# Where RMSNorm's 1/rms is applied in a one-core hybrid layer: on x before its transposes, or on q, k, v and the LRU's tiles after the projection

## What is computed

```
h    = x * rsqrt(mean(x*x) + eps) * mix_norm_g          # RMSNorm per token
proj = h @ w_in                                         # 1024 -> 2560
xr, yg, q, k, v = split(proj)                           # 512 channels each
xr   = causal_conv4(xr) + b                             # per channel, along tokens
y_lru = rg_lru(xr) * gelu(yg)                           # gates, scan along tokens
q, k = rms_norm(q), rms_norm(k)                         # per head of 64
y_attn = attention(q, k, v)                             # 8 heads, ALiBi slopes
x = x + concat(rms_norm(y_lru), rms_norm(y_attn)) @ w_out
```

## Time and profile before

| what | value |
|---|---|
| median of three runs | 306.27 us |
| span of the profiled execution, first to last instruction | 304.5 us |
| what lies around the span, against the median of the runs | 1.8 us |
| PE busy | 298.2 us (98%) |
| DVE busy | 231.5 us (76%) |
| ACT busy | 175.8 us (58%) |
| transfers | 52.20 MB, mean 171 GB/s |

### The profile page before, as it was taken

How to read it: one execution, slowest core, us unless ns; L and a number is a source line. 1 busy time by engine, 2 the same in 40 slices (tenths; PEclk the granted TensorE clock), 3 DMA queues, 4 the chain that set the end, 5 groups by cost and what they waited for, 6 DMA issues and landing times.

```text
span 304.5 us, 5577 instructions
## 1 busy us (share of the span) xinstructions
PE 298.2 (98%) x2008; PEld 274.0 (90%) x2008; DVE 231.5 (76%) x410; ACT 175.8 (58%) x304; POOL 4.0 (1%) x21
## 2 busy tenths in 40 slices
PE   8899999999999999999999999999999999999995
PEld 8788998898988789999999999999999999999994
DVE  2998597798799767887787778777777778777765
ACT  6975598997756376854445545555444544555420
POOL 4000000000000000000000000000000000000000
PEclk9999999999999999999999999999999999999999
DMA  7999943033307701655365455355464554300003
GB/s 229 425 420 424 377 145 138 2 138 138 140 9 263 282 2 23 238 208 225 140 220 194 144 194 213 140 212 199 146 243 161 157 223 171 138 0 0 0 0 139
DMA packets 7981, 52.20 MB, mean 171 GB/s; under 512 B 896, under 2 KB 896, under 8 KB 2080
## 3 DMA queue, kind: packets, MB, share of 16 engines
q1 hardware_dynamic: 7776, 51.38, 45.4%
q0 software_dynamic: 192, 0.64, 0.5%
HBM read 50.98 MB, written 1.05 MB: 171 GB/s over the span
## 4 chain that ended last, share of the span: by engine, by line
PE 93%; DMA 2%; DVE 2%; ACT 1%; issue 0%; SPq 0%; ACTq 0%
PE bank L901 29%; PE bank L902 28%; PE bank L905 28%; DMA raw<-in_stream_dram 2%; PE bank L977 1%; DVE x_tok L893 1%; PE bank L990 1%; PE bank L1096 1%; PE bank L1095 1%; PE bank L966 1%; PE bank L1089 1%; PE bank L997 1%; PE bank L998 1%; PE bank L1115 0%; ACT p_T L498 0%
## 5 line engine op out<-in xcount | busy, mean ns | idle before, releaser
L901 PE MATMUL bank<-h_hi,w_hi 128*128 128x256 f32 x416 | 118.3, 284 | 0.3 <-DVE h_lo L823 0.3
L905 PE MATMUL bank<-h_hi,w_lo 128*128 128x256 f32 x416 | 117.7, 283 | 0.0
L902 PE MATMUL bank<-h_lo,w_hi 128*128 128x256 f32 x416 | 117.7, 283 | 0.0
L590 DVE TENSOR_TENSOR w_lo<-raw,w_hi 128x1024 fp32r<-128x1024 f32 x93 | 112.3, 1217 | 3.3 <-ACT w_hi L321 3.1
L321 ACT ACTIVATE w_hi<-raw 128x1024 fp32r<-128x1024 f32 x87 | 90.8, 1051 | 2.7 <-PE bank L905 1.8
L901 PEld LDWEIGHTS bank<-h_hi,w_hi 128*128 128x128 f32 x416 | 79.7, 192 | 3.0 <-issue 1.8
L902 PEld LDWEIGHTS bank<-h_lo,w_hi 128*128 128x128 f32 x416 | 79.7, 192 | 0.8
L905 PEld LDWEIGHTS bank<-h_hi,w_lo 128*128 128x128 f32 x416 | 79.7, 192 | 0.0
L543 ACT ACTIVATE xc<-bank,par 128x256 f32<-128x256 f32 x44 | 24.9, 566 | 87.7 <-PE bank L905 87.7
L849 DVE SCALAR_TENSOR_TENSOR xc<-bank,par,xc 128x255 f32<-128x255 f32 x44 | 21.2, 482 | 34.5 <-ACT xc L543 34.5
L901 PE MATMUL bank<-w_hi,act_hi 128*128 128x512 f32 x88 | 34.6, 393 | 0.0
(11 more groups left out here) (156 smaller groups left out, 302.6 us busy)
## 6 DMA issues: line engine op xcount, KB each, us to landing
raw<-in_stream_dram SPq DMA_DIRECT2D x46, 1024.0 KB, 4.8
x_tok<-in_x_dram SPq DMA_DIRECT2D x2, 512.0 KB, 3.8
raw<-in_stream_dram SPq DMA_DIRECT2D x2, 512.0 KB, 7.2
out_dram<-x_tok SPq DMA_DIRECT2D x4, 256.0 KB, 2.0
p_T<-in_gates_dram POOLq DMA_DIRECT2D x1, 512.0 KB, 9.3
par<-in_params_dram POOLq DMA_DIRECT2D x1, 117.0 KB, 4.6
```

The source lines that it names most:

```text
L590: dve.tensor_tensor(w_lo[u % RING][:, :], raw_unit(u), w_hi[u % RING][:, :].bitcast(F32), ALU.subtract).then_inc(lo_done, 1)
L901: pe.matmul(acc, lhs_hi, rhs_hi, start=first, stop=False)
L902: pe.matmul(acc, lhs_hi, rhs_lo, start=False, stop=False)
L905: return pe.matmul(acc, lhs_lo, rhs_hi, start=False, stop=last)
```

## The change

The x tiles are transposed as they land. The chunks `h_hi`, `h_lo` carry the gain but not the inverse rms. The sums of squares become mean squares on DVE after unit 1, ACT takes both roots behind unit 1 of its list, DVE makes the reciprocals and two diagonal tiles behind unit 3. Between the q and the k units PE multiplies ones by the diagonals, which spreads the inverse rms as a row over all partitions (bank 7); ACT copies it to `x_rows`. In q's and k's norm the scale cancels but for epsilon, so epsilon becomes a bias per token, eps * (mean square), with one root per 128 tokens in place of one per 256. The copy of v takes the inverse rms as its scale. The X and Y tiles are multiplied by `x_rows` on DVE: the X tiles go from PSUM to `x_scaled` ahead of all taps of their convolution, the Y tiles to `ygate` ahead of gelu. The first transfer of the stream is cut from 1024 to 512 columns, and the rest of the first two units comes in one transfer of 1536 columns, for which ACT's half of unit 0 now waits. The warm-up has 7 products in place of 14.

```
-WARM_UP = 14
+WARM_UP = 7
+HEAD = 512
...
-            sp.dma_start(raw[0][:, 0:UNIT], stream[0, :, 0:UNIT]).then_inc(first_landed, 16)
-            sp.dma_start(raw[0][:, UNIT:2 * UNIT], stream[0, :, UNIT:2 * UNIT]).then_inc(raw_landed[0], 16)
+            sp.dma_start(raw[0][:, 0:HEAD], stream[0, :, 0:HEAD]).then_inc(first_landed, 16)
+            sp.dma_start(raw[0][:, HEAD:2 * UNIT], stream[0, :, HEAD:2 * UNIT]).then_inc(raw_landed[0], 16)
...
 # ACT
             h_part(0)
-            act.wait_ge(first_landed, 16)
-            act.activation(w_hi[0][:, 512:UNIT], raw[0][:, 512:UNIT], ACT.Copy).then_inc(hi_done, 1)
+            act.wait_ge(raw_landed[0], 16)
+            act.activation(w_hi[0][:, HEAD:UNIT], raw[0][:, HEAD:UNIT], ACT.Copy).then_inc(hi_done, 1)
             h_part(1)
             h_part(2)
             his(1)
+            act.wait_ge(x_ms_done, TT)
+            act.activation(x_rms, x_ms, ACT.Sqrt).then_inc(x_rms_done, 1)
             for kc in (3, 4, 5):
                 h_part(kc)
...
-                act.activation(qk_rms[:, g:g + TT, :], qk_ss[:, g:g + TT, :], ACT.Sqrt, bias=eps,
-                               scale=1.0 / HEAD_DIM).then_inc(qk_rms_done, 1)
+                for m in range(TT):
+                    act.activation(qk_rms[:, g + m, :], qk_ss[:, g + m, :], ACT.Sqrt, bias=qk_bias[:, m:m + 1],
+                                   scale=1.0 / HEAD_DIM).then_inc(qk_rms_done, 1)
 
             def conv_first(c):
-                act.wait_ge(unit_used, U_X + c + 1)
+                act.wait_ge(x_scaled_done, c + 1)
...
-                act.activation(xc[:, c, :], X_ACC[c][:, 0:SEQ], ACT.Identity, bias=par[:, CONV_B + c:CONV_B + c + 1],
+                act.activation(xc[:, c, :], x_scaled[c], ACT.Identity, bias=par[:, CONV_B + c:CONV_B + c + 1],
...
             roots(0)
+            act.wait_ge(x_spread, 1)
+            act.activation(x_rows[:, :], X_ROWS, ACT.Copy).then_inc(x_rows_done, 1)
...
-                act.activation(v_tok[:, m, :], V_ACC[m][:, :], ACT.Copy).then_inc(v_ready, 1)
+                act.activation(v_tok[:, m, :], V_ACC[m][:, :], ACT.Copy,
+                               scale=x_rstd[:, m:m + 1]).then_inc(v_ready, 1)
 # DVE
+            def x_mean_squares():
+                dve.wait_ge(x_sq, TT)
+                dve.tensor_scalar(x_ms[:, 0:1], x_ss[:, 0:1], 1.0 / D_MODEL, EPS, ALU.mult, ALU.add).then_inc(x_ms_done, 1)
+                dve.scalar_tensor_tensor(x_ms[:, 1:2], x_ss[:, 1:2], 1.0 / D_MODEL, x_mean, ALU.mult,
+                                         ALU.add).then_inc(x_ms_done, 1)
+                dve.wait_ge(x_ms_done, TT)
+                dve.tensor_scalar(qk_bias, x_ms, EPS, None, ALU.mult).then_inc(qk_bias_done, 1)
...
+            def x_scale(c):
+                dve.wait_ge(unit_used, U_X + c + 1)
+                dve.wait_ge(x_rows_done, 1)
+                dve.tensor_tensor(x_scaled[c], X_ACC[c][:, 0:SEQ], x_rows[:, :], ALU.mult).then_inc(x_scaled_done, 1)
+
+            def y_scale(j):
+                dve.wait_ge(unit_used, U_Y + 2 * j + 2)
+                dve.tensor_tensor(ygate[:, 2 * j:2 * j + 2, :], Y_ACC[j][:, :].rearrange("p (c t) -> p c t", c=2),
+                                  x_rows[:, :].unsqueeze(1).to_broadcast([P, 2, SEQ]), ALU.mult).then_inc(y_scaled, 1)
...
             los(1)
+            x_mean_squares()
...
             los(3)
+            x_diagonals()
...
             los(12, 13)
+            x_scale(0)
+            x_scale(1)
             conv_rest(0)
             conv_rest(1)
             los(14)
             shift(0)
             shift(1)
+            x_scale(2)
             conv_rest(2)
             los(15)
+            x_scale(3)
             shift(2)
             shift(3)
             conv_rest(3)
...
             shift(6)
             shift(7)
+            y_scale(0)
             los(19, 20)
+            y_scale(1)
 # PE
-                pe.wait_ge(x_normed[m], 2)
+                pe.wait_ge(x_landed[m], 16)
...
                 rows_unit(U_Q + j, U_Q, Q_ACC, hT_lo)
+            pe.wait_ge(x_diag, TT)
+            for m in range(TT):
+                ins = pe.matmul(X_ROWS[:, P * m:P * (m + 1)], ones[:, :], diag[:, m, :], start=True, stop=True)
+            ins.then_inc(x_spread, 1)
```

More of the change, by code:

```diff
@@ L135, in build_layer @@
         x_norm = [flat(decay), flat(gate_i)]
+        x_scaled = [gate_i[:, c, :] for c in range(LC)]
         sq_tok = flat(p_T)[:, 2560:3072]
@@ L163, in build_layer @@
         dist_done = sem("dist_done")
-        warm, x_normed = sem("warm"), [sem(f"x_normed{m}") for m in range(TT)]
+        warm = sem("warm")
+        x_diag, x_spread, x_rows_done = sem("x_diag"), sem("x_spread"), sem("x_rows_done")
+        x_ms_done, qk_bias_done, x_scaled_done, y_scaled = (
+            sem("x_ms_done"), sem("qk_bias_done"), sem("x_scaled_done"), sem("y_scaled"))
         first_hi, first_lo = sem("first_hi"), sem("first_lo")
-        x_sq, x_sq_1 = sem("x_sq"), sem("x_sq_1")
+        x_sq = sem("x_sq")
         own_hi, q_scale_done, f_added = sem("own_hi"), sem("q_scale_done"), sem("f_added")
-        x_rms_done, x_rec = sem("x_rms_done"), sem("x_rec")
+        x_rms_done = sem("x_rms_done")
         xT, hT_hi, hT_lo = sem("xT"), sem("hT_hi"), sem("hT_lo")
@@ L332, in _ @@
             act.activation(flat(ygate), x_tok[:, 0, :], ACT.Square, accum_out=x_ss[:, 0:1]).then_inc(x_sq, 1)
[L333 to L343, removed]
-            act.wait_ge(x_landed[1], 16)
[L346 to L351, removed]
+            act.wait_ge(x_landed[1], 16)
+            act.activation(flat(decay)[:, 0:512], x_tok[:, 1, 512:1024], ACT.Square, accum_out=x_ss[:, 1:2]).then_inc(x_sq, 1)
             def h_part(kc):
@@ L614, in _, with x_diagonals @@
             link(dve.tensor_tensor_reduce(flat(tanh_a)[:, 0:512], half, half, 1.0, 0.0, ALU.mult, ALU.add, x_part))
-            dve.tensor_scalar(x_mean, x_part, 1.0 / D_MODEL, EPS, ALU.mult, ALU.add).then_inc(x_sq_1, 1)
-            x_scale(0)
-            x_reciprocal(1)
-            x_scale(1)
+            link(dve.tensor_scalar(x_mean, x_part, 1.0 / D_MODEL, EPS, ALU.mult, ALU.add))
+            def x_mean_squares():
[5 more added lines that the diff above has]
+                dve.tensor_scalar(qk_bias, x_ms, EPS, None, ALU.mult).then_inc(qk_bias_done, 1)
+            def x_diagonals():
+                dve.wait_ge(x_rms_done, 1)
+                link(dve.reciprocal(x_rstd, x_rms))
+                dve.wait_ge(consts, 2)
+                for m in range(TT):
+                    dve.tensor_scalar(diag[:, m, :], ident[:, :], x_rstd[:, m:m + 1], None, ALU.mult).then_inc(x_diag, 1)
+            def x_scale(c):
[6 more added lines that the diff above has]
+                                  x_rows[:, :].unsqueeze(1).to_broadcast([P, 2, SEQ]), ALU.mult).then_inc(y_scaled, 1)
             def h_part(kc):
@@ L669, in conv_rest @@
                     col = CONV_W + (LRU_CONV - 1 - back) * LC + c
-                    tap = dve.scalar_tensor_tensor(xc[:, c, back:SEQ], X_ACC[c][:, 0:SEQ - back],
+                    tap = dve.scalar_tensor_tensor(xc[:, c, back:SEQ], x_scaled[c][:, 0:SEQ - back],
                                                    par[:, col:col + 1], xc[:, c, back:SEQ], ALU.mult, ALU.add)
```

29 lines of the change are left out of this document (13 added, 16 removed).

## The result

| | kernel before | changed kernel |
|---|---|---|
| median of the runs | 306.37 us (305.87 to 306.62, 4 runs) | 315.25 us (313.71 to 318.29, 4 runs) |
| span of the profiled execution | 304.5 us | 313.8 us (its time 315.56 us) |
| mean granted clock, profiled | 0.999 | 0.984 |
| share of the chain on PE | 93% | 85% |

The changed kernel takes 1.0304 times as long (95% interval 1.0266 to 1.0342). The prediction said 313.3 us, and 310.2 to 315.8. Its four runs lie 4.6 us apart, those of the kernel before 0.8, and the higher ones have the lower mean clock: 313.71 us at 0.989, 314.93 at 0.988, 315.56 (the profiled one) at 0.984, 318.29 at 0.978.

The account below looks back on a forecast made before the run. PE, with 93% of the chain, was taken as the bound. Delays of 1.5 + 0.5 + 1.2 + 2.2 + 0.3 + 1.3 = 7.0 on a span of 304.5, plus 1.8 to the median, gave 313.3 us (310.2 to 315.8).

Parts of the forecast that it names:

- What bounds the kernel: Whole kernel: time of PE's first product, PE's work and its waits; x's normalisation is not in the chain.
- Halving them saves at least 0.6 and at most 1.3; I take 1.0.: Stream's first transfer, 512 KB cut to 256 KB: PE's first product moves from 10.30 to about 9.3.
- The start, 1.5: Up to unit 2: ACT's half of unit 0 waits for the second transfer, delaying PE's unit 2 by 1.5 us.
- pauses before chunk 1, unit 1 and unit 2: At the start: PE, unpaused before, now pauses at these three places and loses its gain at the first product.
- The spread row, 0.5: Between q and k: two products of ones by a diagonal add 0.5 us to PE's stream.
- The X tiles, 1.2: Before score 0: X products queue behind units 12 and 13 on DVE, delaying ACT's taps and copies; PE stalls 1.2 us.
- convolution 3, 2.2: Before the fourth pair of gate products: PE stalls 2.2 us for convolution 3, late through the ACT and DVE queues.
- The transposes of the probabilities, 0.3: At these transposes: PE waits for the last of eight late sigmoids on ACT, 0.3 us more.
- v, 1.3: Before P times V: Y products and late ACT and DVE delay the copy of v; PE waits 1.3 us.
- The second rival: First products: PE starts at the lower clock, between nothing and +2.8 us; 314.7 us, chance 0.14.
- The first and third rivals: First: stream lands earlier, 311.5 us, chance 0.13. Third: queues in the middle looser than read, 309.0 us, chance 0.07.
- The fourth: Faster: first product 1.0 earlier and kept, second transfer landing before 8.3, X products under cover; 305.8 us, chance 0.05.

Follow-up runs that it names:

- b_early: b_all with six chunks on ACT and four on DVE done before the first weights land, 7 warm-up products before x's transposes and 8 behind: 306.49 us.
- d_first: Changed kernel with the stream's first transfer (256 KB) issued ahead of x: 320.37 us, one run.
- s_warm14: Changed kernel with 14 warm-up products again in place of 7: 314.33 us, ratio 1.0259.
- m_order: Changed kernel with only DVE's list reordered, X products 0 and 1 ahead of splits 12 and 13, 2 ahead of 14, 3 ahead of 15: 309.83 us.
- m_fill4: Changed kernel with 12, 5, 9 and 5 unused products of ones in PE's four pauses: 314.16 us, ratio 1.0236.
- c_start: Changed kernel with first two transfers and ACT's wait as before, root behind unit 3, 14 warm-up products; middle left as changed: 313.70 us.
- b_all: Changed kernel with c_start's start, m_order's DVE list, and ACT's copies of v ahead of its table load: 306.92 us, ratio 1.0017.
- m_fill: Changed kernel with 12 unused products of ones on PE ahead of the last pair of gate products: 318.62 us.
- s_root: Changed kernel with ACT's root moved behind unit 3 and DVE's mean squares behind unit 2: 314.93 us, one run.
- s_split: Changed kernel with the first two transfers of 1024 columns again and ACT's half of unit 0 waiting for the first: 318.16 us, ratio 1.0377.

## Why the prediction was right in its time, and where not in its steps

**What bounds the kernel.** Right. x's normalisation was not on the chain, and its removal moved nothing: the first product is at 10.34 for 10.30. What stood in the chain was chunk 0's `h_lo` (0.41), and the change makes it possible to take that out, as b_early did.

**"Halving them saves at least 0.6 and at most 1.3; I take 1.0."** Failed. It saved 0.04 between these two executions, and 0.2 between the means of six and six. The step took 205 GB/s for a property of the stretch, by which half the bytes take half the time. d_first shows a time that comes with the stream's first transfer, and that rows half as long don't shorten by much. The error did little, since the gain was written off against later pauses anyway.

**The start, 1.5; measured 2.0.** The mechanism was right in each link: ACT's half behind the second transfer, then 2.31 to the end of unit 1's rounding (forecast 2.30), the wait at the root, PE at unit 2 by DVE's split. The mis-sized term is the landing of the second transfer: 10.45, not 9.9. It scatters: in the six profiled executions with this transfer behind x, ACT begins its half between 9.85 and 10.55. Each link behind it stands 0.3 to 0.6 later than forecast, the split's end at 17.67 for 17.25. The forecast's pauses before chunk 1, unit 1 and unit 2 are in s_warm14 (PE goes on at 12.17, 13.89 and 17.56). In the changed kernel itself they hardly show, because the low clock had made PE as late as its operands; that the start costs 2.0 there and not more is a coincidence of the two.

**The spread row, 0.5.** Right: 0.44 in the chain, 0.5 between the table's rows.

**The X tiles, 1.2; convolution 3, 2.2.** Right: 1.3 and 2.3, and m_order shows the queue in front of the products as the cause, by removing both with no operation less. Each link can be read in the chain above; the X product was put at 0.45 and took 0.42.

**The transposes of the probabilities, 0.3.** 0.5 at the full clock: the place is right, the size 0.2 short.

**v, 1.3.** Measured 1.34 in m_fill4, but 0.1 in the changed kernel. There PE was late already, and v was ready when it came: a term that failed in this kernel, because of another that was left out.

**What was left out: the clock.** The sum at full clock is 8.0 us, forecast 7.0. The changed kernel's execution has 9.3. The difference of 1.3 to 1.4 is the clock: its fall behind the pause of 2.1 us costs 2.7 at the transposes of the probabilities (9.2 - 6.6), of which the vanished wait for v gives back about 1.2. The prediction put a price on the lower clock only at the first products, and none on the pauses that it forecast itself. The median is 2.0 above 313.3: 1.0 by sizes (by m_fill4 0.6 at the start and 0.4 in the rest), and about as much by this. That the median lies in the range is in part luck: the 2.8 that stretched it to 315.8 were there for a low clock at the first products, where it turned out hidden, and one of the four runs, 318.29, lies outside.

**The second rival** took the Trainium skill's "TensorE: Matmul & The Clock Gate", Part 4: PE-mode transpose, by which transposes do not count as PE being busy, to mean first products at 1.2 GHz. This case's traces don't bear that out, and d_first settles it. There the transposes come late, PE runs nothing else between 4.4 and 11.0 us, and from the second on they start 0.21 us apart, the last at 10.12:

```profile
6.90 3.50 PE L978 MATMUL bank<-ident,x_tok 128*128 128x128 f32 x16 [2.46 <-DMA x_tok<-in_x_dram]
11.01 0.47 PE L919 MATMUL bank<-w_hi,h_hi 128*128 128x512 f32 x1 [0.61 <-DVE h_lo L632]
```

In the changed kernel they are 0.11 apart from 4.6 us on. So in d_first they ran at the lower level, and the first products behind them, 0.23 apart from 11.32 on, ran at the higher one: the clock rose behind transposes alone. (The profile's clock column doesn't tell this. It has no record before 10.1 us in d_first and before 4.4 in the changed kernel, and says 1.00 there although the passes are 0.21 apart.) In the changed kernel, with seven warm-up products, the clock was up during the transposes and at the first product:

```profile
4.50:6.50 2.00, 1.88 (x16) 1.53 (x15) 0.85 (x3) 1.82 (x5) 0.43 (x5) 1.00 0.85 197
```

It fell at about 11.3, after the idle time from 6.6 to 10.3 and the first four products. So first products at 1.2 GHz did come, in part, as this rival has it, but behind a pause and not because of the transposes. With 14 warm-up products it stayed up in s_warm14, but fell at 12.0 in c_start and at 11.9 in b_all; with 12 fillers behind the transposes it stayed up (m_fill4). In s_warm14 and m_fill4 the start isn't faster for it (17.56 and 17.83 at unit 2), because DVE's split is the last to be ready.

**The first and third rivals** did not come: the second transfer was later and not earlier, and the queues were as tight as read. **The fourth** needed its landing before 8.3 and failed at 10.45.

## What to carry to other kernels

Price a new operation by what stands ahead of it in its engine's queue when its input is ready, and not by its length: four products of 0.42 us cost 3.6 us behind four splits of 1.2 (two ahead of the first pair, one ahead of each of the others), and nothing ahead of them. A wait that a change puts into PE's stream has a second price, the clock that may fall behind it; forecast it as a range of its own, and fill the pauses with idle products in one variant to read the rest cleanly. Before shortening a transfer, see whether its time is that of its bytes. And before reading a gain of a few tenths from one pair of traces, see how far the first landing scatters between executions: here 8.0 to 9.0.

## What the runs showed of the hardware that was not expected

- A pause of 0.9 to 2.1 us in PE's stream was followed by stretches at 1.2 GHz of some 7 us (59.1 to 65.8 in the changed kernel) and 10 us (89.7 to 99.7 in m_fill), in some executions and not in others: m_fill's four runs had clocks of 0.978, 0.978, 0.979 and 1.000, and took 318.35, 318.89, 319.26 and 313.78 us. The pause of 2.1 us was followed by a fall in the changed kernel, s_root and c_start, and by none in s_split and s_warm14. What tells these executions apart is open. The kernel before, which has no such pause, has 0.993 in a few of its runs (308.37 us).
- The wait for v is short, 0.9 to 1.2, and what follows it are products of 64 columns; the clock fell there in s_split, s_warm14, m_fill and m_order, which all came to it early. Those products alone don't do it: in m_fill4, with fillers in the wait, and in the changed kernel, with no wait there, the same products ran with the clock up.
- The stream's first transfer cost about 2 us whether its 128 rows are 2 or 4 KB, and wherever in the order it is asked for: 90 GB/s at 3.0 us in d_first, with 343 at 4.5, and 90 at 6.0 in the changed kernel, with 401 at 7.5. The transfers behind it have over 400.
- PE's clock rose behind transposes alone: in d_first PE had been idle from 4.4 to 6.9 us and then ran nothing but 16 transposes, and the clock was up at about 10.1 us, where its clock record begins.
